# Router by column groups, state transposes in a gap, and two tiles' expert rows added by adding transfers: a change to a one-core hybrid decoder step

## The chip, the cores and the metric

One core of one Trainium2 chip runs the whole kernel. The metric is device time in microseconds of an execution; lower is better. The kernel before was timed in three runs, and one further execution was taken by the hardware profiler. Times of the trace are microseconds from the start of its span.

## What is computed

One layer over 512 prompt tokens and 32 sample tokens (8 sequences of 4), width 1024, all in float32. Cut to what the change touches:

```python
x = x + g1 * mix                          # mix: pooling and short convolution, then w_out
h2 = rmsnorm(x, norm2) * (1.0 + sc2) + sh2
logits = h2 @ w_router + b_router         # 32 experts
top_v, top_i = lax.top_k(logits, 4)
gates = softmax(top_v)
# every expert: down(((u + 1) * g * sigmoid(1.702 g))) + b_down on the rows that chose it
ffn = zeros.at[token].add(y_rows * gate)  # four rows a token
x = x + g2 * ffn
y = rmsnorm(x, final_norm)
```

Beside y it returns the last 15 rows of the pooling input and the last 2 rows of the convolution input, for the prompt and for the samples (the "states").

## The kernel before

The tokens are five tiles: four of 128 prompt tokens (t = 0 to 3) and one of 32 sample tokens (t = 4, `PT`). Each engine has its own program in a block of the dense part (to about 250 us) and in a block of the experts; they meet at semaphores, and within an engine the order is the written one. That order, not a planner, sets when things run.

**Dense part.** TensorE multiplies the output projection tile by tile (`mix(t)`, L1096, samples at L1092). VectorE gates and adds it into `x_sb` (L892, L893), ScalarE squares and takes the root, VectorE normalises into `h_row` (L741, L743), TensorE transposes that (`transposes`, L955) and ScalarE copies it out of PSUM as `h_t` (`turned`, L537). `router(t)` (L1108) multiplies `h_t` as the loaded operand, eight chunks of 128 by 128 tokens, with the 32 columns of `wr_sb`. A float32 product is two records in the trace. `best(t)` on VectorE (L866 to L874) adds the bias, takes the top 8, their indices, casts these to float (`top_f`, L870), and makes one-hot rows and a mask. The order on TensorE is h0, mix(2), h1, router(0), mix(3), h2, router(1), transposes of the prompt's last state columns into `acc_u` (L1139, L1141), mix(4), h3, router(2), router(3), the samples' rows, router(4), ranks (L1159 to L1163), transposes of the samples' state columns (L1168, L1170). `TP` names the uses of the PSUM buffer `tp` in order: TensorE counts `tp_full`, ScalarE `tp_free`. The normalised rows are stored to DRAM (`h2_dram`), tiles 0 to 2 by SP, tile 3 and the samples by ScalarE's queue.

**Experts.** An expert takes up to 96 rows of the normalised tokens (3 blocks `b` of 32), each row cut into 4 quarters that lie on the four groups of 32 partitions; TensorE works on four column groups at once. `row_ids(e)` (L2088) gives the indices of expert e's rows, VectorE's `ids(e)` (L1718 to L1723) turns them into addresses, and GpSimd gathers (L1549) one block at a time; VectorE transposes the rows (`turn_first` for expert 0 by block, L1735; `turn_rows`, L1742 and later). The first two experts get their indices in this way, the others from a table made of ranks and gates: pairs (L1892, L1905) on VectorE, `values_by_rank` (L2097) on TensorE, more of VectorE (to L1926), `values_by_slot` (L2105). TensorE's order at the start is row_ids(0), row_ids(1), g2 of the prompt (L2179), g2 of the samples (L2182), `keep_clock` (L2112, a product nobody reads), gate and up of expert 0 (L2124, L2146), values_by_slot, gate and up of expert 1. From there the loop is gate_up(i) (L2146, 192 records), down(i) (L2171, 192 records).

Weights go through 12 slots of 1 MB, in pairs of 2 MB from expert 1 on, on SP's queue (L1468), each load waiting for TensorE to have used the slots. Expert outputs, scaled by gate and g2, are scattered by GpSimd (L1562) as quarter rows into `expert_rows` in DRAM (`y_dram`), row 4 * token + k for the token's k-th choice. The outputs of the last two experts (`LATE`) stay in SBUF.

**End.** When all scatters but those of the last two experts have landed, SP loads the rows back (L1493, L1497): tiles 0 and 1 as `picked[0]`, `picked[1]` (2 MB each, a token's four rows side by side in one partition), tile 2, the samples and tile 3 with one row a partition into free weight slots. Tiles 0 and 1 are summed by VectorE (`add_pairs` L1788, `add_rows` L1793 and L1795), in its program around the last expert's `y_add` (L1772, L1776). TensorE takes the last two experts' rows to their tokens with a 0/1 matrix (`late_expert`, L2258, 48 records a tile) and, for tiles 2, 3 and the samples, adds the loaded rows by products with `sel_4`, which sums four neighbouring partitions (`other_experts`, L2269 to L2276). The tile order is `SEQUENCE = [0, 1, PT, 2, 3]`. VectorE adds each result to `x_sb` (`add_tile`, L1815; tile 3 by quarters, L1802), ScalarE squares (L1670), VectorE scales by `final_norm` (L1981, L1996), and the tiles are stored. `late_expert(3)` waits for the samples' root, since that sum and tile 3 share a PSUM bank.

Of the kernel before, what the change touches and what calls it, by code (L numbers as in the profile page):

```python
# [6 lines left out]
ALU = mybir.AluOpType  # L7
# [45 lines left out]
Q = 4  # L53
# [11 lines left out]
def hybrid_step(nc, x_prompt, x_sample, state_pool, state_conv, c_prompt, c_sample, norm1, norm2,  # L65
# [11 lines left out]
    with top:  # L77
# [127 lines left out]
        v_new = sb("v_new", [P, GR, DEC_B * CPAST])  # L205
        logit = sb("logit", [P, TT, E])
        top_i = sb("top_i", [P, TT, 8], U32)
        top_f = sb("top_f", [P, TT, TOPK])
# [27 lines left out]
        rank_ps = acc_y[:, 0, PT * E:(PT + TT) * E].rearrange("p (t e) -> p t e", e=E)  # L236
        ss_ps = acc_g[:, 1, 0:1]
# [17 lines left out]
        consts = sem("consts")  # L255
# [43 lines left out]
        TP += ["pm_s", "h0", "h1", "h2", "h3", "h4"]  # L299
# [85 lines left out]
        def _(sp):  # L385
# [23 lines left out]
            sp.wait_ge(so0_full, 1)  # L409
            sp.wait_ge(new_packed, 4)  # L410
# [6 lines left out]
        def _(pool):  # L417
# [9 lines left out]
            pool.memset(eps_c[:, :], EPS).then_inc(consts, 1)  # L427
            pool.memset(ss[:, :], 1.0).then_inc(consts, 1)
# [23 lines left out]
            for w in range(16):  # L452
                pool.memset(inv_n[:, w:w + 1], 1.0 / (w + 1)).then_inc(consts, 1)
            pool.memset(uext[:, :, 0:PAST], 0.0).then_inc(consts, 1)
            pool.memset(vext[:, :, 0:CPAST], 0.0).then_inc(consts, 1)
            pool.memset(top_v[:, :, :], 0.0).then_inc(consts, 1)
# [75 lines left out]
        def _(act):  # L532
# [28 lines left out]
            act.wait_ge(consts, 2)  # L561
# [95 lines left out]
            def states(i0, src):  # L657

                for i in (i0, i0 + 1):
# [8 lines left out]
                           vext_s[:, :, :, DEC_T:DEC_T + CPAST], ACT.Copy).then_inc(new_packed, 1)  # L668
            for t in range(PT):
# [8 lines left out]
                if t == 0:  # L678
# [11 lines left out]
            act.activation(rstd_q[:, :], ss_ps, ACT.Sqrt, bias=eps_c[:, 0:1], scale=1.0 / D).then_inc(sq_done, 1)  # L690
            store(PT - 1)
            empty(f"h{PT}", h_t[:, :, SEQ:NTOK].rearrange("p (q h) s -> p h q s", q=Q),
                  tp[:, 0, 0:QW].rearrange("p (h q s) -> p h q s", h=KT // Q, q=Q))
            act.wait_ge(h_ready, TT + PT + 1)
# [14 lines left out]
        def _(dve):  # L709
# [79 lines left out]
            dve.wait_ge(consts, CONSTS)  # L789
# [72 lines left out]
            def best(t):  # L862
# [57 lines left out]
        def _(pe):  # L920
# [179 lines left out]
            def router_part(t, lo_, hi_):  # L1100
                r = norm_rows(t)
                out_ = lg[t]
                if lo_ == 0:
                    pe.wait_ge(tp_free, TP[f"h{t}"] + 1)
                    if t >= 2:
                        pe.wait_ge(logits_in, t - 1)
                for k in range(lo_, hi_):
                    mm = pe.matmul(out_, h_t[:, k, t * P:t * P + r], wr_sb[:, k, :],  # L1108
                                   start=(k == 0), stop=(k == KT - 1))
                if hi_ == KT:  # L1110
                    mm.then_inc(lg_done, 1)

            def router(t):
                router_part(t, 0, KT)
# [15 lines left out]
            transposes("h1", 1, TT)  # L1130
            router(0)
            mix(3)
            transposes("h2", 2, TT)
            router(1)
            pe.wait_ge(pm_ready, 2 * GR)
            pe.wait_ge(conv_s_ready, GR)
            pe.wait_ge(x1_ready, PT)
            for g in range(GR):
                pe.transpose(acc_u[0:PAST, 0, g * P:(g + 1) * P], uext[:, g, SEQ:SEQ + PAST], ident[:, :])  # L1139
            for g in range(GR):  # L1140
                mm = pe.transpose(acc_u[0:CPAST, 1, g * P:(g + 1) * P], vext[:, g, SEQ:SEQ + CPAST], ident[:, :])  # L1141
            mm.then_inc(so0_full, 1)
            mix(4)
            transposes("h3", 3, TT)
            router_part(2, 0, KT // 2)
            pe.wait_ge(act_step, 2 * TT)
            pe.matmul(ss_ps, same_s[:, :], ss_q[:, 0:1], start=True, stop=True).then_inc(ss_summed, 1)
            router_part(2, KT // 2, KT)
            router(3)
            take("h4")  # L1150
# [4 lines left out]
            router(4)  # L1155
# [10 lines left out]
            pe.wait_ge(new_packed, 4)  # L1166
            for g in range(GR):
                pe.transpose(tp[0:NS, 0, g * P:(g + 1) * P], u_new[:, g, :], ident[:, :])  # L1168
            for g in range(GR):
                mm = pe.transpose(tp[0:DEC_B * CPAST, 1, g * P:(g + 1) * P], v_new[:, g, :], ident[:, :])  # L1170
            mm.then_inc(so_full, 1)
# [30 lines left out]
        with ExitStack() as experts:  # L1202
# [93 lines left out]
            quarter_done = sem("quarter_done")  # L1296
# [121 lines left out]
            picked_at = [picked[0], picked[1]] + [slots(n, 2).rearrange("p (k d) -> p k d", k=TOPK) for n in (0, 4, 6)]  # L1418
# [24 lines left out]
            def _(sp):  # L1443
# [37 lines left out]
                for t in (0, 1, 2, PT, 3):  # L1481
# [4 lines left out]
                    if t == 2:  # L1486
                        sp.wait_ge(mm_done, pos(E - 1, 2 * MCH - 1) + 1)
# [43 lines left out]
            def _(pool):  # L1531
# [7 lines left out]
                def gather_waits(e):  # L1539

                    pool.wait_ge(id_ready, e + 1)
                    if not (isinstance(e, int) and e == 0):
                        pool.wait_ge(ht_ready, e)
# [158 lines left out]
            def _(dve):  # L1702
# [94 lines left out]
                def add_tile(t):  # L1797
# [14 lines left out]
                    if t < AHEAD:  # L1812
                        dve.wait_ge(x_added, t + 1)
# [518 lines left out]
```

## Time and profile before

| | us |
|---|---|
| median of 3 runs | 1278.76 (1278.58 to 1279.07) |
| the profiled execution's own time | 1278.6 |
| its span in the trace | 1276.8 |
| TensorE busy | 1259.5 |
| VectorE busy | 522.0 |
| GpSimd busy | 250.0 |
| ScalarE busy | 92.8 |

In the rows, PE is TensorE's matmuls and PEld its loads of the stationary operand (the first shape in a row is that of the loaded operand), DVE is VectorE, ACT ScalarE, POOL GpSimd, SPq the DMA queue of SP. q1 is SP's hardware queue, q0 the one that GpSimd issues to. A row of the timeline merges instructions of one line that follow each other (x, a count); in square brackets stands the idle time of the engine before it and what ended it. Ends of matmuls are modelled, so starts are the surer numbers. The chain that ended last is followed back from the last instruction, each time to what released it.

### The profile page before, as it was taken

How to read it: one execution, taken by the hardware profiler on the slowest of the kernel's cores; microseconds unless marked ns; L12 is line 12 of the kernel's file. 1: busy time of each engine (PE TensorE's matmuls, PEld its weight loads, DVE VectorE, ACT ScalarE, POOL GpSimd, SP SyncE). 2: the span in 40 equal slices, each digit the busy share in tenths (PEclk: the TensorE clock that was granted, in tenths of full speed). 3: DMA queues.
4: the chain of work that ended last, by engine and by line, in shares of the span. 5: the costliest groups of instructions: out<-in, count | busy, mean ns of one | idle time of the engine just before them, and what ended most of it. 6: DMA issues, size and time to landing. Idle time of an engine off the chain costs nothing.

```text
span 1276.8 us, 32305 instructions
## 1 busy us (share of the span) xinstructions
PE 1259.5 (99%) x14181; PEld 587.5 (46%) x14181; DVE 522.0 (41%) x826; ACT 92.8 (7%) x184; POOL 250.0 (20%) x333
## 2 busy tenths in 40 slices
PE   8999999899999999999999999999999999999997
PEld 7777755533344334433443444444444444333445
DVE  2033323575333333333333344444444444444346
ACT  5110011200000000000000000000000000000002
POOL 4502300122222111111221111111111111112110
PEclk9999999799999999999999999999999999999999
DMA  9455968399999999999999999999999999999994
GB/s 349 138 210 214 354 247 335 101 392 426 423 428 428 426 427 426 425 428 425 428 424 424 428 424 419 426 426 427 423 417 429 424 424 429 422 425 427 426 423 176
DMA packets 62819, 487.60 MB, mean 382 GB/s; under 512 B 10563, under 2 KB 19635, under 8 KB 37441
## 3 DMA queue, kind: packets, MB, share of 16 engines
q1 hardware_dynamic: 47826, 455.79, 85.6%
q0 software_dynamic: 11632, 20.85, 4.6%
q10 hardware_dynamic: 3327, 10.47, 2.1%
q8 instruction: 25, 0.41, 0.1%
q14 instruction: 9, 0.07, 0.0%
HBM read 468.48 MB, written 25.88 MB: 387 GB/s over the span
## 4 chain that ended last, share of the span: by engine, by line
PE 94%; DVE 3%; DMA 1%; issue 1%; POOL 0%; ACT 0%; POOLq 0%; DVEq 0%; ACTq 0%
PE acc L2146 50%; PE acc L2171 24%; PE acc L1004 9%; PE acc L1096 4%; PE acc L934 2%; DMA rows<-h_rows,row_first 1%; PE acc L2258 1%; PE acc L978 1%; PE acc L955 1%; DVE picked L1788 0%; PE acc L1068 0%; PE acc L1092 0%; PE acc L1108 0%; POOL rows L1549 0%; PE acc L2273 0%
## 5 line engine op out<-in xcount | busy, mean ns | idle before, releaser
L2146 PE MATMUL acc<-raw,ht 128*32 128x512 f32 x2928 | 319.8, 592 | 0.0
L2146 PE MATMUL acc<-raw_b,ht 128*32 128x512 f32 x2928 | 319.8, 592 | 0.0
L1851 DVE TENSOR_TENSOR g_sb<-acc,bias_gu 128x768 f32<-128x768 f32 x32 | 30.7, 958 | 518.0 <-PE acc L2146 518.0
L1549 POOL DMA_INDIRECT rows<-h_rows,row_next x90 | 93.4, 1037 | 689.1 <-DVE row_next L1729 625.2
L2146 PEld LDWEIGHTS acc<-raw_b,ht 128*32 128x32 f32 x2928 | 95.0, 110 | 219.1 <-issue 219.1
L2146 PEld LDWEIGHTS acc<-raw,ht 128*32 128x32 f32 x2928 | 95.1, 110 | 205.7 <-issue 200.4
L2171 PE MATMUL acc<-raw_b,at 128*32 128x256 f32 x2976 | 166.3, 379 | 0.0
L2171 PE MATMUL acc<-raw,at 128*32 128x256 f32 x2976 | 166.3, 379 | 0.0
L2171 PEld LDWEIGHTS acc<-raw_b,at 128*32 128x32 f32 x2976 | 96.7, 110 | 77.1 <-issue 18.6
L2171 PEld LDWEIGHTS acc<-raw,at 128*32 128x32 f32 x2976 | 96.7, 110 | 63.9
L1004 PE MATMUL acc<-h_t,raw 128*128 128x256 f32 (+1 forms) x512 | 119.8, 395 | 0.4 <-DVE h_t L764 0.3
L1004 PEld LDWEIGHTS acc<-h_t,raw 128*128 128x128 f32 x512 | 96.6, 190 | 22.4 <-issue 2.6
L1562 POOL DMA_INDIRECT expert_rows<-y_sb,y_idx x90 | 91.6, 1018 | 75.1 <-DVE y_sb L1776 47.7
L1631 ACT ACTIVATE a_sb<-g_sb 128x768 f32<-128x768 f32 x32 | 27.1, 846 | 603.3 <-DVE g_sb L1853 603.3
L1751 DVE STREAM_TRANSPOSE at<-a_sb 128x768 f32<-128x768 f32 x31 | 49.7, 1603 | 27.6 <-PE acc L2171 27.6
L1742 DVE STREAM_TRANSPOSE ht<-rows 128x768 f32<-128x768 f32 x30 | 48.0, 1601 | 0.8 <-DMA rows<-h_rows,row_next 0.8
L1762 DVE TENSOR_SCALAR weight<-g_q,table 128x256 f32<-128x256 f32 x96 | 33.8, 408 | 4.9 <-issue 4.9
L1624 ACT ACTIVATE y_idx<-table,q_col 128x3 uint32 (+1 forms) x30 | 9.0, 298 | 318.5 <-DVE y_sb L1772 318.5
L1776 DVE TENSOR_TENSOR y_sb<-y_sb,weight 128x768 f32<-128x768 f32 x31 | 29.7, 959 | 3.5
L1863 DVE SCALAR_TENSOR_TENSOR a_sb<-u_sb,g_sb 128x768 f32<-128x768 f32 x32 | 30.7, 959 | 1.1
L1859 DVE TENSOR_TENSOR g_sb<-g_sb,a_sb 128x768 f32<-128x768 f32 x32 | 30.5, 952 | 0.0
L1854 DVE TENSOR_TENSOR u_sb<-acc,bias_gu 128x768 f32<-128x768 f32 x32 | 30.4, 951 | 0.0
(296 smaller groups left out, 694.4 us busy)
## 6 DMA issues: line engine op xcount, KB each, us to landing
raw<-in_w_down SPq DMA_DIRECT2D x33, 2048.0 KB, 16.9
raw<-in_w_gate SPq DMA_DIRECT2D x31, 2048.0 KB, 11.7
raw<-in_w_up SPq DMA_DIRECT2D x31, 2048.0 KB, 16.1
raw_b<-in_w_gate SPq DMA_DIRECT2D x31, 2048.0 KB, 11.2
raw_b<-in_w_up SPq DMA_DIRECT2D x31, 2048.0 KB
raw_b<-in_w_down SPq DMA_DIRECT2D x31, 2048.0 KB, 16.5
raw<-in_w_ada SPq DMA_DIRECT2D x24, 1024.0 KB, 10.5
expert_rows<-zeros ACTq DMA_DIRECT2D x1, 8704.0 KB, 29.0
```

What stands on the lines that cost most here:

```text
L1004: mm = pe.matmul(z_half(f, b), w[:, j, (f % 2) * P:(f % 2 + 1) * P], h_t[:, j, lo_:hi_], start=(j == 0), stop=(j == KT - 1))
L1096: mm = pe.matmul(out_[0:r, h, :], mix_t[j][:, t * P:t * P + r], w[:, j % KC, h * HALF:(h + 1) * HALF], start=(j == GR), stop=(j == GR - 1))
L1549: pool.indirect_dma_start(rows[:, b, :], None, h2_quarter, bass.IndirectOffsetOnAxis(ap=idx[:, b:b + 1], axis=0), bounds_check=Q * NTOK - ...
L1562: pool.indirect_dma_start(y_quarter, bass.IndirectOffsetOnAxis(ap=y_idx[:, b:b + 1], axis=0), y_sb[:, b, :], None, bounds_check=Q * ROWS - ...
L1742: dve.transpose(ht_of(e)[:, :, :, :], turned(rows)).then_inc(ht_ready, 1)
L1751: dve.transpose(at_[:, :, :, :], turned(a_sb)).then_inc(at_ready, 1)
L1762: dve.tensor_scalar(weight[:, b, :], g2_q[:, :], in_prompt, in_sample, ALU.mult, ALU.add)\
L1851: dve.tensor_tensor(g_sb[:, :, :], gate_of(i, 0), plus(0), ALU.add).then_inc(g_read, 1)
L1859: dve.tensor_tensor(g_sb[:, :, :], g_sb[:, :, :], s_sb[:, :, :], ALU.mult).then_inc(glu_done, 1)
L1863: dve.scalar_tensor_tensor(out=a_sb[:, :, :], in0=u_sb[:, :, :], scalar=1.0, in1=g_sb[:, :, :], op0=ALU.add, op1=ALU.mult).then_inc(act_re ...
L2146: mm = pe.matmul(gu_of(i)[b][q * TB:(q + 1) * TB, :].rearrange("p (m n) -> p m n", m=2), ht_of(i)[:, b, k, :], w[:, kk, :, q * CW:(q + 1) ...
L2171: mm = pe.matmul(out_[q * TB:(q + 1) * TB, b, :], x[:, b, k, :], w[:, kk, q * CW:(q + 1) * CW], start=(k == 0), stop=(k == KT - 1))
```

## The change

- Router: `router_parts(t)` loads `wr_sb` chunks (32 columns) as the stationary operand into column group k mod 4 and moves `h_t` (128 tokens) past it, giving four partial sums of 32 logits in the four partition groups. ScalarE copies them (`partial_sums`), and `router_fold(t)` sums the four groups with one product with `same_s`. `TP` gets the names r0 to r4. The fold stands behind the next tile's transposes.
- `best(t)` compares with the integer indices and has no cast.
- The prompt's last state columns are copied by ScalarE into `end_cols`; their transposes and those of the samples' states move from the dense part to behind row_ids(0), ahead of row_ids(1). `keep_clock` moves ahead of both g2 products, and g2 of the samples goes between blocks 0 and 1 of expert 0's first products.
- On VectorE the gates subtraction moves behind the members of expert 1, and ids(1) ahead of turn_first. GpSimd's gathers for expert 1 wait for each block of expert 0 to be turned, no longer for all of them.
- Tiles 2 and 3: GpSimd adds the four rows a token straight to `x_sb` with `dma_start(..., accum_op=add)`, eight transfers of 512 KB, each waiting for the one before of its tile; the first two are issued with SP's first loads of the rows, the others behind the last expert's gate and up. SP's loads of these tiles and TensorE's `other_experts` for them go; tile 3 is added whole and no longer by quarters.
- The semaphore `consts` is merged into `rows_cleared`; SP waits for six packings before its third load of experts.

```diff
@@ ScalarE, dense part
+            def partial_sums(t):
+                empty(f"r{t}", part_sb[t], part_ps[t])
...
+            act.activation(end_cols[:, :, 0:PAST], uext[:, :, SEQ:SEQ + PAST], ACT.Copy).then_inc(new_packed, 1)
+            act.activation(end_cols[:, :, PAST:PAST + CPAST], vext[:, :, SEQ:SEQ + CPAST], ACT.Copy)\
+                .then_inc(new_packed, 1)
...
+                if t:
+                    partial_sums(t - 1)
                 if t < PT - 1:
                     turned(f"h{t}", t)
@@ TensorE, dense part
+            def router_parts(t):
+                r = norm_rows(t)
+                pe.wait_ge(tp_free, TP[f"h{t}"] + 1)
+                if t >= 2:
+                    pe.wait_ge(logits_in, t - 1)
+                for k in range(KT):
+                    g = k % Q
+                    mm = pe.matmul(part_ps[t][g * E:(g + 1) * E, :], wr_sb[:, k, :], h_t[:, k, t * P:t * P + r],
+                                   start=(k < Q), stop=(k >= KT - Q))
+                mm.then_inc(tp_full, 1)
+            def router_fold(t):
+                pe.wait_ge(tp_free, TP[f"r{t}"] + 1)
+                pe.matmul(lg[t], part_sb[t], same_s[:, 0:E], start=True, stop=True).then_inc(lg_done, 1)
...
             mix(2)
-            transposes("h1", 1, TT)
-            router(0)
+            router_parts(0)
+            row_transposes(1)
+            router_fold(0)
             mix(3)
...
@@ VectorE, best(t)
-                step(dve.tensor_copy(top_f[0:r, t, :], top_i[0:r, t, 0:TOPK]))
                 step(dve.tensor_tensor(onehot[0:r, t, :, :], iota_e[0:r, :].unsqueeze(1).to_broadcast([r, TOPK, E]),
-                                       top_f[0:r, t, :].unsqueeze(2).to_broadcast([r, TOPK, E]), ALU.is_equal))
+                                       top_i[0:r, t, 0:TOPK].unsqueeze(2).to_broadcast([r, TOPK, E]), ALU.is_equal))
@@ SP, end
-                for t in (0, 1, 2, PT, 3):
+                for t in (0, 1, PT):
...
-                    if t == 2:
-                        sp.wait_ge(mm_done, pos(E - 1, 2 * MCH - 1) + 1)
@@ GpSimd, experts
+                    if isinstance(e, int) and e == 1:
+                        pool.wait_ge(first_turned, b + 1)
...
+                def add_rows(t, k):
+                    rows_ = y_dram[TOPK * P * t:TOPK * P * (t + 1), :].rearrange("(p k) d -> k p d", k=TOPK)
+                    if k:
+                        pool.wait_ge(rows_added[t - AHEAD], 16 * k)
+                    pool.dma_start(x_sb[:, t, :], rows_[k], accum_op=ALU.add).then_inc(rows_added[t - AHEAD], 16)
+
+                pool.wait_ge(y_stored, 16 * SB * (E - LATE))
+                for t in range(AHEAD, PT):
+                    add_rows(t, 0)
                 pool.wait_ge(mm_done, pos(E - 1, 2 * MCH - 1) + 1)
                 pool.iota(tokno, pattern=[[Q, NTOK]], base=0, channel_multiplier=0,
                           allow_small_or_imprecise_dtypes=True).then_inc(numbered, 1)
+                for k in range(1, TOPK):
+                    for t in range(AHEAD, PT):
+                        add_rows(t, k)
@@ VectorE, add_tile(t)
-                    if t == LAST:
-                        for q in range(Q):
-                            dve.wait_ge(quarter_done, q + 1)
...
+                    else:
+                        dve.wait_ge(rows_added[t - AHEAD], 16 * TOPK)
@@ TensorE, start of the experts
                 row_ids(0)
+                end_states()
+                sample_states()
                 row_ids(1)
+                keep_clock()
                 pe.wait_ge(so_ready, 4)
...
-                keep_clock()
                 gate_up_first()
```

## Rows read from the trace of the kernel before

**Rows 1.** The page, part 1: busy time, share of the span, instructions, per engine.

```profile
PE 1259.5 (99%) x14181; PEld 587.5 (46%) x14181; DVE 522.0 (41%) x826; ACT 92.8 (7%) x184; POOL 250.0 (20%) x333
```

**Rows 2.** Waits of SP's queue, 290 to 1240 us: us in total, times, longest.

```profile
SPq L1468 <- PE acc L2146: 570.9, 61, 12.0
```

**Rows 3.** Chain, 200 to 340 us: start, us, engine and line, instructions.

```profile
214.16 1.71 PE acc L1108 x16
...
233.38 3.64 PE acc L1092 x64
...
246.29 0.85 PE acc L1168 x4
...
248.00 0.62 PE acc L2088 x44
...
279.81 20.74 PE acc L2146 x192
```

**Rows 4.** Timeline, 237 to 248 us: start, us, instruction, [idle before, releaser].

```profile
237.04 0.42 DVE L905 TENSOR_TENSOR h_q<-acc,g_q 128x256 f32<-128x256 f32 x1 [0.30 <-PE acc L1092]
...
240.98 0.17 DVE L870 CAST top_f<-top_i 128x4 f32<-128x4 uint32 x1
...
242.20 0.19 DVE L866 TENSOR_TENSOR logit<-acc,br_bc 128x32 f32<-128x32 f32 x1 [0.31 <-DVE mask_bf L874]
...
246.78 0.66 DVE L1712 TENSOR_TENSOR member<-iota_m,rank_m 128x480 bf16<-128x480 f32 x1
```

**Rows 5.** Windows: start:end, length, TensorE busy us, clock share, DMA share, GB/s.

```profile
252.00:256.00 4.00, 4.00 (x18) 0.53 0.37 105
```

**Rows 6.** Timeline, 254 to 279 us.

```profile
254.22 11.23 PE L2124 MATMUL acc<-raw_b,ht 128*32 128x512 f32 x96
...
262.48 4.16 DVE L1905 TENSOR_TENSOR picked<-onehot,pair_v 128x3840 bf16<-128x3840 f32 x1
...
263.09 4.43 POOL L1549 DMA_INDIRECT rows<-h_rows,row_first  x1 [0.30 <-issue]
...
273.51 1.61 DVE L1742 STREAM_TRANSPOSE y_sb<-rows 128x768 f32<-128x768 f32 x1 [6.87 <-DMA rows<-h_rows,row_first]
...
278.90 0.91 PE L2105 MATMUL acc<-picked,sel_r 96*128 96x96 f32 x6 [1.23 <-DVE picked L1926]
```

**Rows 7.** Timeline, 1248 to 1270 us.

```profile
1248.00 2.29 DVE L1788 TENSOR_TENSOR picked<-picked 128x2048 f32<-128x2048 f32 x1
...
1250.20 0.95 DVE L1772 TENSOR_TENSOR u_sb<-acc,bias_d 128x768 f32<-128x768 f32 x1
...
1262.70 1.93 PE L2273 MATMUL acc<-raw_b,sel 128*32 128x256 f32 x32
...
1263.30 0.49 DVE L1996 SCALAR_TENSOR_TENSOR raw<-x_sb,fin_rstd,fn_q 128x256 f32<-128x256 f32 x1
...
1267.37 1.93 PE L2273 MATMUL acc<-raw_b,sel 128*32 128x256 f32 x32
...
1268.15 1.65 DVE L1802 TENSOR_TENSOR x_sb<-x_sb,acc 128x256 f32<-128x256 f32 x4 [0.51 <-PE acc L2273]
```

**Rows 8.** DMA, 1229 to 1234 us; then the queues (packets, MB) 1218.0 to 1219.3.

```profile
DMA packets 147, 2.15 MB, mean 429 GB/s; under 512 B 16, under 2 KB 16, under 8 KB 16
...
q1 hardware_dynamic: 34, 0.51, 91.5%
q0 software_dynamic: 33, 0.08, 15.9%
```

**Rows 9.** Tile `picked`, 1200 to 1277 us: issues, and issue to landing.

```profile
L1493 SPq DMA_DIRECT2D picked<-expert_rows x2: 326/350/373, 1223.0 to 1223.4; - x2
...
DMA to landing us min/median/max: 16.5/18.7/20.9
```

**Rows 10.** Tile `raw`, 1215 to 1225 us: issues, and issue to landing.

```profile
L1468 SPq DMA_DIRECT2D raw<-in_w_down x2: 342/380/418, 1219.1 to 1219.5; - x2
...
DMA to landing us min/median/max: 10.6/12.8/15.1
```

More of the change, by code:

```diff
@@ L236, in hybrid_step @@
         rank_ps = acc_y[:, 0, PT * E:(PT + TT) * E].rearrange("p (t e) -> p t e", e=E)
+        part_ps = [acc_y[:, t % 2, 3 * P:3 * P + (NS if t == PT else P)] for t in range(TT)]
+        part_sb = [gate_c[:, 2 + t % 2, 0:NS if t == PT else P] for t in range(TT)]
         ss_ps = acc_g[:, 1, 0:1]
@@ L1098, in mix, with row_transposes @@
                 mm.then_inc(mix_done, 1)
-            def router_part(t, lo_, hi_):
+            def router_parts(t):
                 r = norm_rows(t)
[L1102 to L1114, printed above, removed]
+                pe.wait_ge(tp_free, TP[f"h{t}"] + 1)
[9 more added lines that the diff above has]
+                pe.matmul(lg[t], part_sb[t], same_s[:, 0:E], start=True, stop=True).then_inc(lg_done, 1)
+            def row_transposes(t):
+                transposes(f"h{t}", t, TT, tp, TP[f"h{t - 1}"] + 1)
             pe.wait_ge(conv_ready, GR - 1)
@@ L1129, in _ @@
             mix(2)
-            transposes("h1", 1, TT)
-            router(0)
+            router_parts(0)
+            row_transposes(1)
+            router_fold(0)
             mix(3)
-            transposes("h2", 2, TT)
-            router(1)
+            router_parts(1)
+            row_transposes(2)
+            router_fold(1)
             pe.wait_ge(pm_ready, 2 * GR)
             pe.wait_ge(conv_s_ready, GR)
[L1137 to L1142, printed above, removed]
             mix(4)
-            transposes("h3", 3, TT)
-            router_part(2, 0, KT // 2)
+            router_parts(2)
+            row_transposes(3)
+            router_fold(2)
             pe.wait_ge(act_step, 2 * TT)
             pe.matmul(ss_ps, same_s[:, :], ss_q[:, 0:1], start=True, stop=True).then_inc(ss_summed, 1)
-            router_part(2, KT // 2, KT)
-            router(3)
-            take("h4")
+            router_parts(3)
+            router_fold(3)
+            pe.wait_ge(tp_free, TP["h3"] + 1)
             pe.wait_ge(h_ready, TT + PT + 1)
@@ L1154, in _ @@
             mm.then_inc(tp_full, 1)
-            router(4)
+            router_parts(4)
+            router_fold(4)
             pe.wait_ge(mask_ready, 1)
@@ L1164, in _ @@
             mm.then_inc(rank_done, 1)
[L1166 to L1171, printed above, removed]
         part.close()
@@ L1295, in hybrid_step @@
             tile_done = sem("tile_done")
-            quarter_done = sem("quarter_done")
+            rows_added = [sem(f"rows_added{t}") for t in range(2)]
             fin_cross = sem("fin_cross")
@@ L1414, in blocks @@
                     again()
-            picked_at = [picked[0], picked[1]] + [slots(n, 2).rearrange("p (k d) -> p k d", k=TOPK) for n in (0, 4, 6)]
+            picked_at = {0: picked[0], 1: picked[1], PT: slots(6, 2).rearrange("p (k d) -> p k d", k=TOPK)}
             beside = slots(2, 2)
@@ L1541, in gather_waits @@
                     pool.wait_ge(id_ready, e + 1)
-                    if not (isinstance(e, int) and e == 0):
+                    if not isinstance(e, int) or e > 1:
                         pool.wait_ge(ht_ready, e)
@@ L1873, in _ @@
                 dve.wait_ge(rows_zeroed, 16)
-                dve.tensor_tensor(gates[:, :, :], top_v[:, :, 0:TOPK], top_v[:, :, 0:1].to_broadcast([P, TT, TOPK]),
-                                  ALU.subtract).then_inc(shifted, 1)
                 chain(dve.scalar_tensor_tensor(out=rank_m[:, :, :], in0=rank_ps, scalar=1.0, in1=mask_bf[:, :, :],
@@ L1882, in _ @@
                 members(1)
+                dve.tensor_tensor(gates[:, :, :], top_v[:, :, 0:TOPK], top_v[:, :, 0:1].to_broadcast([P, TT, TOPK]),
+                                  ALU.subtract).then_inc(shifted, 1)
                 chain(dve.tensor_tensor(pick[:, :, :, :], onehot[:, :, :, :],
@@ L2180, in _ @@
                 mm.then_inc(g2_spread, 1)
-                for q in range(Q):
-                    mm = pe.matmul(g2_s_ps[q * NS:(q + 1) * NS, :], sel_s[:, q, :], mod_g2[:, :], start=True, stop=True)
-                mm.then_inc(g2_spread, 1)
-                keep_clock()
                 gate_up_first()
```

82 lines of the change are left out of this document (45 added, 37 removed).

## The prediction

> **What bounds the kernel now.** The page first: TensorE has work in 99% of the span and VectorE in 41% [rows 1]. Weights stream all the while too, so the wait table of SP's own queue has to say who paces whom: through the experts the weight loads wait for TensorE's matmuls to free a slot [rows 2], and in the table of the engines TensorE waits for no load. An expert's gate and up are 20.74 us of products back to back [rows 3]; the change touches neither these nor the down products. It can act only where the chain leaves them: between the output projection and expert 1's first product (214 to 280 us), and behind the last down product (1250 us on). I read the chain of waits there, then the timeline for what stands beside it.
>
> **Front, step by step.**
>
> 1. Router. A tile's 8 products take 1.71 us on the chain, 16 records that each load 128 columns [rows 3]. `router_parts` loads 32 columns, four groups at once, with 128 moving columns. Nearest is mix(4): 64 such records with 256 moving columns in 3.64 us, 0.057 each. 16 of them give 0.91, half of that if the moving columns set it; I take 0.6. The fold adds two records at the old price (0.11 each): 0.2. So a tile saves 0.9 (0.6 to 1.05). The ACT copy between is hidden by the next row transposes and an idle ACT; without that cover it would cost its own 0.3.
> 2. Only router(0) stands ahead of mix(3), so tile 3's sum starts 0.9 earlier; `best(1)` on VectorE's way loses its cast (0.17 and 0.03 of issue), 1.1. Before, VectorE waited 0.30 at L905 for mix(4) [rows 4]; mix(4) moves up by two router tiles, 1.8, and by the state transposes, so the wait goes and VectorE leads. h_q: 1.4 earlier.
> 3. `best(2)` to `best(4)` follow back to back: three casts, 0.6, and the 0.3 of idle at 242.20 [rows 4]. The masks are ready 2.3 earlier.
> 4. Expert 0's members are made at 247.44 [rows 4], but their ids start at 248.00, behind two groups of transposes of 0.85 each [rows 3], which now stand behind them: 0.5. The gates subtraction leaves this path too, which I count as nothing. The first gather goes out 2.8 earlier; its rows are turned at about 251.1.
> 5. What is late next is TensorE: 0.62 of ids, then 16 transposes (twice the two groups, 3.4), ids(1) 0.6 to 0.8, `keep_clock` and g2 of the prompt (1.7 and 0.85 at the slow clock, half at the full one). From 245.2 that ends between 251.2 and 252.6. First product at 251.9 against 254.22: 2.3 gained, bounds 1.6 and 3.1. SP's loads of slots 4 and 5 start behind the first gathers and move up with them; 10 us of products cover them.
> 6. Clock. Between 252 and 256 the grant was 0.53 of full, that is mostly 1.2 GHz [rows 5], after the router steps in which VectorE leads and TensorE waits. The first 96 records took 11.23 us [rows 6] where 96 of the same shape take 10.37 (half of 20.74): 0.9 lost. With TensorE busy from 245 on I expect it back (bounds 0 and 0.9). Against it g2 of the samples enters the products: 0.43.
> 7. Expert 1's gathers were asked for at 258.5; the third one's issue alone took 4.43 us beside a 4.16 us product of pairs on VectorE, its rows came at 273.5, and TensorE stood 1.23 us before L2105 [rows 6]. With ids(1) ahead of `turn_first` the indices are there at about 250.4 (when row_ids(1) leaves TensorE), and the gathers follow block by block; with the same landing of some 10 us they are there by 268. VectorE then reaches the slot values near 270, TensorE needs them at 275. The 1.23 goes.
>
> Front: 2.3 + 0.9 - 0.4 + 1.2 = 4.0 us; with the bounds of steps 1, 5 and 6, 2.4 to 4.8. The copies into `end_cols`, the merged semaphore and SP's wait for six packings hang on engines long idle there: nothing.
>
> **Tail, the gain.** other_experts(2) and the quarters of tile 3 leave TensorE (1.9 each). Tile 3's late products ran from 1264.6 to 1267.4, VectorE's last quarter ended at 1269.80 [rows 7]. Now they wait for the samples' root (1263.1) and end at 1265.9, and VectorE is what is late: samples finished at 1263.8 [rows 7], add of tile 2 1.22, weighting 1.23, root and reciprocal to 1266.8, add of tile 3 1.22: 1268.0. Gain 1.8; what follows is unchanged.
>
> **Tail, the price.** GpSimd issues eight adding transfers of 512 KB, two at once with SP's loads of `picked` (1223.0), the others from 1230, each behind its tile's last. SP's two 2 MB loads for tiles 2 and 3 go, but they were queued behind both picks and delayed nothing; the adds are on a queue of their own. Where both queues had work, 34 packets went on one and 33 on the other: turn by turn [rows 8]. A 16 KB packet of the stream costs an engine 0.61 us (131 in 5 us on 16 engines: 147 less the 16 small ones) [rows 8], one of 4 KB a quarter of that, 0.15. From the first add to the second pick's landing, 1244.2 [rows 9], the stream sends some 30 packets an engine, and a 4 KB row of the adds goes behind each. Who waits: add_pairs(1) on VectorE starts at 1248.00, 3.8 us behind that landing, and right behind it is the last expert's y_add, which today starts the moment the last down product is out (1250.20) [rows 7]. Every microsecond beyond 3.8 delays the end.
>
> No row shows an adding packet. Lower bound: a plain one, 0.15, 4.5 in all, 0.7 beyond the slack (none at all is a rival below). Upper bound: x is read as well, so two reads of 4 KB, 0.30: 9.0, 5.2 beyond. A plain packet is the nearest row, the second read is the nearest mechanism; I take the middle, 0.22: 6.6, 2.8 beyond. By then four adds are done; the rest run alone at some 5 us a pair and end near 1260, ahead of 1263.8. The weights of the last down products landed by 1234.6 [rows 10]; these products end at 1250.2 and take half of an expert's gate and up, so they need them from 1239.8 on: covered, 3 us later too.
>
> **Sum.** -4.0 - 1.8 + 2.8 = -3.0 on the profiled execution's 1278.6 (span 1276.8); the median of the runs is 0.16 above it, 1278.76: 1275.7.
>
> **A rule against the change.** GpSimd's issue was held for 4.43 us beside VectorE's tensor_tensor [rows 6], so an add's issue beside add_pairs (2.3) may be held as long. While the queue is full that is hidden; it counts for the third rival. The Trainium skill (SBUF — State Buffer, "Who interferes with whom") infers that tensor_tensor leaves descriptor writing alone and that copies and tensor_scalar lock it out. By its inference that issue would not have been held; the row decides.
>
> **Rivals.**
> - *The picks are not late* (0.18). If the adds get less than every second turn, the slack covers them: -4.0 - 1.8, 1272.9. For: adds of one tile are chained, so their queue may run dry. Against: two tiles interleave, and the other queue's packets did get every turn.
> - *Adds too dear, slower* (0.25). Place: add_pairs(1) waiting for `picked[1]`. From 0.32 us an adding packet the whole gain is gone; at 0.45 (row read, x read, x written one after another) the delay is 13.5, 9.7 beyond the slack: 1278.8 - 5.8 + 9.7 = 1282.7.
> - *The adds themselves late* (0.12). If a 4 KB row goes as several packets, each waits its own 0.61 us: at two, 10 to 12 us a transfer, two are done by 1247, six remain in three rounds of 5 to 6 us, 1263 to 1266. With picks little delayed that is 1 to 3 us late: 1274 to 1276. The Trainium skill (DMA: Bandwidth & Descriptors, "Anatomy of one DMA") fits 2.0 us plus bytes at 436 GB/s; an estimate by it is 3.2 us per add, the last one near 1243, and nobody would wait for it.
> - *The front gives less* (0.10). ids(1) now holds `turn_first` on VectorE until TensorE is through 3.4 us of transposes; if these run late and the clock stays low, the front gives 2: 1277.7.
>
> The forecast has 0.35. 0.2% is 2.6 us, about what a measurement of this kernel can tell from no change. Faster: two thirds of the forecast (0.23; its own range is 1273.5 to 1278.5, the bounds of the packet and some of the front's), the first rival, most of the third: 0.51. Slower: nearly all of the second: 0.24. Between: 0.25. The range takes 1272.9 from the first rival and 1282.7 from the second.
>
> **What would show it.** L905 at 235.6; the first L2124 record between 251 and 253 and a full grant before 256; no idle before the slot values; expert 1's first L2146 near 275.8. In the tail, `picked` landing in 21 and 27 us instead of 16.5 and 20.9; VectorE idle before add_pairs(1), y_add 2.8 later against the last down product; no wait for `rows_added`. The prediction is wrong if VectorE waits at `rows_added`, if the picks land in time, or if TensorE waits for a load of the last expert.

## The result, and the profile after

The changed kernel takes **1281.82 us** (median of 11 runs, 1280.19 to 1282.33) beside 1278.77 us for the kernel before (1277.97 to 1279.45) on the same chip: ratio 1.0021, 95% interval 1.0013 to 1.0029. Forecast were 1275.7 us, and faster. The profiled execution has a span of 1279.6 us, against 1276.8 before: +2.8.

**The front did what was forecast, less 0.6 us.** The chain of waits of the changed kernel, 200 to 340 us (start, duration, engine and line, instructions), answers to [rows 3] and, at `h_q`, to the first row of [rows 4]:

```profile
235.58 0.43 DVE h_q L915
...
239.47 0.64 PE acc L1126 x2
...
245.57 0.62 PE acc L2127 x46
...
250.26 1.76 PE acc L2151 x2
...
252.59 3.43 PE acc L2165 x32
...
276.38 20.74 PE acc L2187 x192
```

Expert 1's first product starts at 276.38 where it started at 279.81: 3.43 gained, 4.0 forecast. Through the 30 experts that follow the gain neither grows nor shrinks, since nothing in them was changed. Three rows from the timeline of the same kernel (start, duration, instruction, idle time before it and its releaser) answer to [rows 4] and [rows 6]; the fourth is from the table of windows (length, busy of PE, PEld, DVE, ACT, POOL, then granted clock, DMA share, GB/s) and answers to [rows 5]:

```profile
242.24 0.18 DVE L877 TENSOR_TENSOR logit<-acc,br_bc 32x32 f32<-32x32 f32 x1 [0.52 <-PE acc L1126]
...
256.03 2.46 POOL L1557 DMA_INDIRECT rows<-h_rows,row_first  x1 [0.31 <-issue]
...
264.51 1.61 DVE L1764 STREAM_TRANSPOSE y_sb<-rows 128x768 f32<-128x768 f32 x1 [0.90 <-DMA rows<-h_rows,row_first]
...
252.00:256.00 4.00, 4.00 (x45) 1.41 (x48) 2.87 (x5) 1.50 (x2) 3.12 (x4) 1.00 0.46 114
```

The reader is to see three things: the grant is full from 252 on where it was 0.53 up to 256; the third gather of expert 1 takes 2.46 us to issue and not 4.43; and its rows are turned at 264.5 and not 273.5, so TensorE no longer stops ahead of the slot values.

**The tail gave back twice the gain.** First the timeline of the changed kernel from 1236 us on, which answers to [rows 7]:

```profile
1236.36 0.97 DVE L1794 TENSOR_TENSOR y_sb<-acc,bias_d 128x768 f32<-128x768 f32 x1
...
1242.99 2.29 DVE L1810 TENSOR_TENSOR picked<-picked 128x2048 f32<-128x2048 f32 x1 [3.04 <-DMA picked<-expert_rows]
...
1251.46 2.29 DVE L1810 TENSOR_TENSOR picked<-picked 128x2048 f32<-128x2048 f32 x1 [3.66 <-DMA picked<-expert_rows]
...
1253.67 0.95 DVE L1794 TENSOR_TENSOR u_sb<-acc,bias_d 128x768 f32<-128x768 f32 x1
...
1255.67 2.95 PE L2298 MATMUL acc<-u_sb,raw_b 32*128 32x256 f32 x24 [7.53 <-DVE u_sb L1798]
...
1271.54 1.22 DVE L1832 TENSOR_TENSOR x_sb<-x_sb,acc 128x1024 f32<-128x1024 f32 x1
```

Both `add_pairs` on VectorE wait for their pick, 3.04 and 3.66 us, and the last expert's y_add stands behind the second. Measured from the start of the slot values, y_add comes 1253.67 - 275.47 = 978.2 us later; before it is 1250.20 - 278.90 = 971.3. That is 6.9 us lost, and no other stretch loses as much. Then the landing of `picked` and all packets and the queues from 1225 to 1230 us (packets, MB, share of 16 engines), which answer to [rows 9] and [rows 8]:

```profile
DMA to landing us min/median/max: 23.3/27.3/31.3
...
DMA packets 176, 1.69 MB, mean 338 GB/s; under 512 B 7, under 2 KB 7, under 8 KB 95
...
q1 hardware_dynamic: 88, 1.33, 64.2%
q0 software_dynamic: 88, 0.36, 36.9%
```

88 packets of each queue: turn by turn, as forecast. The 7 packets under 512 B carry almost no bytes; 95 less 7 leaves 88 of 4 KB, which is the whole adding queue. But 36.9% of 16 engines over 5 us is 29.5 us for 88 adding packets, **0.34 us each**, above even my upper bound of 0.30. The count was right. From the first adding packet (1224.1) to the last 16 KB packet of the picks (1249.15) the adding queue moved 1.98 MB, that is 484 packets of 4 KB or 30 an engine, as forecast.

The sum in the trace: first product -3.4, y_add behind it +6.9, and from y_add to the end 25.9 us where it was 26.6, -0.7: +2.8, the difference of the spans.

### The profile page after: what moved, and what is told of

Same layout as the page of the kernel before. It is cut to its first block, busy times and chain, and to the rows that moved or that the text cites. A ratio compares the mean times of both kernels' runs of the same rounds, so it can differ in the third digit from the quotient of the medians.

```text
span 1279.6 us, 32201 instructions
## 1 busy us (share of the span) xinstructions
PE 1252.9 (98%) x14127; PEld 583.9 (46%) x14127; DVE 520.1 (41%) x818; ACT 94.3 (7%) x191; POOL 255.3 (20%) x341
## 4 chain that ended last, share of the span: by engine, by line
PE 93%; DMA 4%; DVE 1%; ACT 1%; issue 1%; SPq 0%; POOL 0%; DVEq 0%; POOLq 0%; ACTq 0%
PE acc L2187 49%; PE acc L2212 24%; PE acc L1014 9%; PE acc L1106 4%; DMA picked<-expert_rows 2%; PE acc L944 2%; PE acc L2298 1%; PE acc L2165 1%; DMA x_sb<-in_x_prompt 1%; DMA expert_rows<-y_sb,y_idx 1%; PE acc L965 0%; PE acc L1078 0%; ACT junk L558 0%; DVE x_sb L1832 0%; ACT raw L1692 0%
## 5 line engine op out<-in xcount | busy, mean ns | idle before, releaser
L1798 DVE TENSOR_TENSOR y_sb<-y_sb,weight 128x768 f32<-128x768 f32 x31 | 29.7, 958 | 3.5
## 6 DMA issues: line engine op xcount, KB each, us to landing
raw_b<-in_w_down SPq DMA_DIRECT2D x31, 2048.0 KB, 17.7
```

## Experiments

Each ratio is against the kernel before on the same chip. "y_add" is the last expert's y_add counted from the start of the slot values, as above; 971.3 is on time.

**1 and 2. The change cut in two.** `front_only` has the hunks of routing and gap and keeps the tail of the kernel before, with tiles 2 and 3 loaded by SP and added by TensorE; `tail_only` has only the new tail, shown here in part, and the merged semaphore:

```
-                for t in (0, 1, 2, PT, 3):
+                for t in (0, 1, PT):
...
+                pool.wait_ge(y_stored, 16 * SB * (E - LATE))
+                for t in range(AHEAD, PT):
+                    add_rows(t, 0)
...
+                for k in range(1, TOPK):
+                    for t in range(AHEAD, PT):
+                        add_rows(t, k)
```

> The changed kernel with the end of the kernel before: tiles 2 and 3 loaded by SP and added by TensorE, no adding transfers. My theory: the front of the change is worth what its trace shows, 3.4 us (expert 1's first product at 276.4 in place of 279.8), and the loss is all in the tail: 1275.3 us against 1278.8. Rival (the shifted front makes the tail late, for instance because weights of the last experts come closer to their use): 1278 or more.

> The kernel before with the new end alone (adding transfers, whole tile 3), and the merged semaphore. My theory: the adds hold back the loads of picked by 7 and 10 us of which 3.8 are covered, so y_add of the last expert comes 6.9 us late; of the 1.8 us that the end gains, 1.3 go to a halved clock of the first late products: +6.4, 1285.2 us. Rival (front and tail hurt one another): about 1280, with the rest of the loss seen only in the two together.

Measured: front alone 1274.50 us, ratio 0.9970 (0.9958 to 0.9981); tail alone 1283.59, ratio 1.0038 (1.0025 to 1.0050). So -4.1 and +5.0; together +0.9, where the whole change measures +3.0. Of the 2.1 between them the traces show 1.0: the front gains 4.1 in `front_only` and 3.4 in the whole change, and y_add is 6.6 late in `tail_only` and 6.9 there; the rest is within the intervals. For the tail alone I had expected 6.4; its trace shows 6.0 (span 1282.8), in an execution 1.0 above the median of its runs. With the front alone the first product starts at 275.69, y_add is on time, and the picks land after 17.2, 19.4 and 21.7 us. The tail alone shows the whole loss by itself:

```profile
DMA to landing us min/median/max: 22.4/26.6/30.8
...
1254.41 2.29 DVE L1799 TENSOR_TENSOR picked<-picked 128x2048 f32<-128x2048 f32 x1 [4.02 <-DMA picked<-expert_rows]
...
1258.62 2.94 PE L2264 MATMUL acc<-u_sb,raw_b 32*128 32x256 f32 x24 [7.20 <-DVE u_sb L1787]
```

**3. Is it the adding, or only the extra transfers?** In `adds_plain` the same eight transfers go at the same places but copy (the addition itself is left out):

```
-                    pool.dma_start(x_sb[:, t, :], rows_[k], accum_op=ALU.add).then_inc(rows_added[t - AHEAD], 16)
+                    pool.dma_start(x_sb[:, t, :], rows_[k]).then_inc(rows_added[t - AHEAD], 16)
```

> The changed kernel with the eight transfers of GpSimd as plain copies into the same tiles of x_sb, same bytes, same places, same waits (tiles 2 and 3 then hold an expert's row instead of x plus four rows). Theory A, the price is the addition: a 4 KB packet costs an engine 0.15 us instead of 0.35, picked lands 3 and 5 us later than before instead of 7 and 10, y_add about 1 us late, the clock stays: 1274.5 to 1275.5 us. Theory B, the price is the turn that any second queue takes from the stream: as the changed kernel, 1281.8 us.

Measured: 1275.69 us, ratio 0.9976 (0.9966 to 0.9985). Landing of `picked`, and all packets and the queues from 1225 to 1230 us:

```profile
DMA to landing us min/median/max: 20.6/23.5/26.3
...
DMA packets 232, 2.06 MB, mean 411 GB/s; under 512 B 30, under 2 KB 30, under 8 KB 132
...
q1 hardware_dynamic: 115, 1.64, 79.5%
q0 software_dynamic: 117, 0.42, 21.1%
```

Here 30 packets are under 512 B, 15 of them in q0, so the copies are 132 less 30, 102 packets of 4 KB. 21.1% of 80 us over 102 is 0.165 us, a little above the lower bound of 0.15. Both queues still take turns, and a turn of the second one costs half of what it does with adds: **an adding packet takes as long as two plain ones of its size**. 1281.82 - 1275.69 = 6.1 us of the kernel's time are due to the adding alone; for the extra transfers as such VectorE still waits 0.43 and 1.30 us for the picks, and y_add is 1.9 late where I had expected about 1.

**4. No adds at all.** `no_adds` is the changed kernel without the eight transfers and VectorE's wait for them (the other experts' rows of tiles 2 and 3 are left out).

> The changed kernel with the eight adding transfers left out (tiles 2 and 3 then lack the rows of the experts but the last two). This has the gain of the tail without its price. My theory: picked lands as before, y_add starts with the last product, late products keep the clock, the end gains the 1.8 us of the prediction: front 3.5 to 4.1 and tail 1.8 below the kernel before, 1272.8 to 1273.4 us. Rival (the new end gains nothing by itself, VectorE's whole adds eat it): as the front alone, 1274.5.

Measured: 1273.31 us, ratio 0.9954 (0.9937 to 0.9970), as expected. The queue from 1225 to 1230 us, the landing, and the last add:

```profile
q1 hardware_dynamic: 150, 2.18, 102.3%
...
DMA to landing us min/median/max: 17.1/19.3/21.5
...
1263.71 1.22 DVE L1824 TENSOR_TENSOR x_sb<-x_sb,acc 128x1024 f32<-128x1024 f32 x1
```

This is the size of the prize: y_add on time, and VectorE's last add ends 1264.93 - 1247.25 = 17.7 us after it, where it was 19.6 before [rows 7]. The tail gain was forecast at 1.8 and is 1.9. The adds cost 1281.82 - 1273.31 = 8.5 us.

**5. Fewer adds, and half adds.** `two_adds` keeps only each tile's first add and leaves out the other six; `adds_half` keeps all eight but moves 512 of the 1024 columns and leaves out the rest:

```
-                    pool.dma_start(x_sb[:, t, :], rows_[k], accum_op=ALU.add).then_inc(rows_added[t - AHEAD], 16)
+                    pool.dma_start(x_sb[:, t, 0:D // 2], rows_[k][:, 0:D // 2],
+                                   accum_op=ALU.add).then_inc(rows_added[t - AHEAD], 16)
```

> Only the first add of each tile is left (two of eight; the other three rows a token of tiles 2 and 3 are left out): 16 adding packets an engine instead of some 27 to 30 ahead of the second pick. Theory A (each adding packet ahead of the picks delays them by its 0.36 us, VectorE has 3 us of slack): second pick lands 27 us after its issue (21.5 + 5.8), y_add 2.5 to 3 us late: 1275.5 to 1277. Theory B (the delay comes from the chained adds that come later, or from something they do to the queue beside their packets): the picks land at 22 us and the time is that without adds, 1273.3.

> Every add moves only the first 512 of the 1024 columns: 2 KB packets instead of 4 KB, as many of them, turn by turn with the stream as before (the second half of the columns of tiles 2 and 3 lacks the rows of the experts). It tells whether the adding packet is paid by its bytes or by its count. Without adds the second pick landed 21.5 us after its issue and the kernel took 1273.3; with the full adds 31.3 us and 1281.8. Theory A, price by bytes (0.36 us at 4 KB, so 0.18 at 2 KB): half the delay, second pick at 26 to 27 us, y_add 2 us late instead of 7: 1275 to 1276.5. Theory B, a fixed price for each packet (0.36 whatever its size): 31 us and 1281 to 1282. Between the two, a fixed part and a part by bytes: the landing tells the split.

Measured, on a chip where the kernel before takes 1280.71 us: 1278.10, ratio 0.9983 (0.9974 to 0.9993), and 1278.18, ratio 0.9983 (0.9973 to 0.9992). The times are above what I expected, for a reason at the front (experiment 9). The part that was to be tested stands in the landings. Of `adds_half`, the landing and the queues from 1236 to 1241 us:

```profile
DMA to landing us min/median/max: 18.5/21.4/24.3
...
q1 hardware_dynamic: 108, 1.61, 76.8%
q0 software_dynamic: 108, 0.22, 23.6%
```

23.6% of 80 us over 108 packets is 0.17 to 0.18 us at 2 KB (one of the 108 is a small one), half of the 0.34 at 4 KB: **an adding packet is paid by its bytes**. The delay fell more than by half (2.8 us and not 4.9). Ordered by it:

| | price of a packet on q0, us | second pick lands after, us | y_add, us |
|---|---|---|---|
| no_adds | none | 21.5 | 971.3 |
| adds_half | 0.18 | 24.3 | 972.0 |
| two_adds | 0.33, half as many | 24.7 | 971.9 |
| adds_plain | 0.165 | 26.3 | 973.2 |
| changed kernel | 0.34 | 31.3 | 978.2 |

The changed kernel run a second time (experiment 9) has its second pick at 32.4 and y_add at 979.4, so a difference of a few tenths between two rows says nothing. Up to a landing of about 24 us less than 1 us is lost; of the 7.0 us by which the second pick comes later in the changed kernel than in `adds_half`, y_add takes over 6.2. `two_adds` fell short of its expected 27 us: 16 packets an engine at 0.33 are 5.3 us, and the pick came 3.2 later. Both the price and the count (256 packets) are in the trace; where the other 2 us went no run shows. In the changed kernel the sum comes out: 30 packets at 0.335 are 10.0 us, and the pick came 9.8 later than without adds.

**6. Could the adds wait until the picks are in?** `adds_last` issues all eight behind both picks' landing; `tile3_adds` is `front_only` with tile 3 alone served by four adds there, tile 2 by TensorE as before. The lines of `adds_last`:

```
+                pool.wait_ge(tile_in[0], 32)
+                pool.wait_ge(tile_in[1], 32)
+                for k in range(TOPK):
```

> The changed kernel with all eight adds issued only when both picked tiles have landed. My theory: picked lands in 16.5 and 20.9 us as before and y_add starts with the last product; the adds then run from about 1241 on without the stream at 0.35 us a packet, four pairs of 6 us, so the last of tile 2 lands near 1263 and of tile 3 near 1266, 2 to 3 us after they are needed: 1276 to 1277 us. Rival (an adding transfer is slow by itself, whatever stands beside it, with 10 us each): 1290 or more.

> The front of the change with adding transfers for tile 3 alone, four of them, issued when both picked tiles have landed; tile 2 is loaded by SP and added by TensorE as before. By the runs so far a chained pair of adds takes 7.4 us without the stream, so one alone some 5: four end near 1262 to 1264, with the load of tile 2's rows beside them; tile 3's late products end near 1263.3. My theory: 0 to 1.1 us under the front alone, 1273.4 to 1274.5 us. Rival (tile 2's rows are held back by the adds as picked was, TensorE waits for them): 1276 or more.

Both expectations missed: 1285.74 us, ratio 1.0054 (1.0037 to 1.0071), and 1282.69, ratio 1.0026 (1.0016 to 1.0036). The second pick landed after 21.5 and 21.8 us and y_add was on time in both. But the chain of adds was last. The timeline of `adds_last`:

```profile
1242.67 1.96 POOL L1617 DMA_DIRECT2D x_sb<-expert_rows  x2 [15.69 <-DMA picked<-expert_rows]
...
1268.54 0.87 POOL L1617 DMA_DIRECT2D x_sb<-expert_rows  x1 [3.18 <-DMA x_sb<-expert_rows]
...
1272.12 1.22 DVE L1831 TENSOR_TENSOR x_sb<-x_sb,acc 128x1024 f32<-128x1024 f32 x1 [11.40 <-DMA x_sb<-expert_rows]
```

Then `tile3_adds`, with the issue to landing of its four adds:

```profile
1266.61 0.87 POOL L1622 DMA_DIRECT2D x_sb<-expert_rows  x1 [6.50 <-DMA x_sb<-expert_rows]
...
1274.02 1.22 DVE L1827 TENSOR_TENSOR x_sb<-x_sb,acc 128x1024 f32<-128x1024 f32 x1 [8.93 <-DMA x_sb<-expert_rows]
...
DMA to landing us min/median/max: 6.6/7.2/8.8
```

I had counted 5 to 6 us for a pair. One add alone takes 7.2 us from issue to landing, a pair 7.4: two in flight cost hardly more than one, so more than half of it is not the packets (8 an engine at the 0.39 that they take alone are 3.1 us) but some 4 us, by subtraction, that every link of the chain pays anew. With four links a tile, that is 30 us. Nobody can wait for that behind the picks. The Trainium skill (DMA: Bandwidth & Descriptors, "Anatomy of one DMA") gives 2.0 us plus bytes at 436 GB/s, 3.2 us for such a transfer by my estimate; the measured 7.2 decides, and the page's fit does not hold for the adding transfers here.

**7. The clock behind the wait.** TensorE stands 7.5 us for y_add, then the 24 records of its first late products take 2.95 us where they took 1.58. `kept_warm` is the changed kernel with 30 products into an unused bank that fill this wait (of their 60 records the trace has 45):

```
+                for _ in range(30):
+                    pe.matmul(psum[:, 3, CW:CW + P], ident[:, :], ident[:, :], start=True, stop=True)
```

> The changed kernel with 30 products of ident on ident, read by nobody, ahead of TensorE's wait for the last y_add, where it now idles 7.5 us. My theory: the grant stays full, the first late products of the last expert take 1.5 us again in place of 2.95, and 1.2 us of the loss come back: 1280.5 us. Rival (the late products were not on the path, VectorE was): 1281.8, no change.

Measured: 1279.42 us, ratio 1.0003 (0.9994 to 1.0013). First the window and the late product of the changed kernel, then, in a second fence, of `kept_warm`:

```profile
1255.00:1257.00 2.00, 1.33 (x12) 1.19 (x16) 1.97 (x3) 0.00 (x0) 0.55 (x1) 0.50 0.84 127
```

```profile
1255.00:1257.00 2.00, 1.30 (x24) 1.25 (x28) 1.97 (x3) 0.00 (x0) 0.53 (x1) 1.00 0.82 129
...
1249.78 5.19 PE L2321 MATMUL acc<-ident 128*128 128x128 f32 x45
...
1255.70 1.58 PE L2298 MATMUL acc<-u_sb,raw_b 32*128 32x256 f32 x24 [0.73 <-DVE u_sb L1798]
```

At a grant of 0.50 (1.2 GHz) 12 records fit where 24 do at 1.00 (2.4 GHz). With the clock kept, VectorE's last add ends 1271.38 - 1253.70 = 17.7 us behind y_add, the same as without adds; in the changed kernel it is 19.1. So the late picks cost 1.4 us a second time, through the clock. The medians differ by more, 2.4 us, but the intervals of the two ratios leave room for 1.4.

**8. Which part of the front carries it?** `ids_back` is `front_only` with `ids(1)` and its gathers where they were, behind `turn_first`:

```
-                ids(1)
                 turn_first()
                 gate_up_bias(0)
+                ids(1)
```

> The front of the change alone, but ids(1) again behind turn_first and the bias, and the gathers of expert 1 behind all blocks. Step 7 of the prediction gave this 1.2 us. My theory: expert 1's rows land some 7 us later than in the front alone, VectorE is late with the slot values and TensorE idles there again, 1.2 us or a little more since TensorE comes 3 us earlier: 1275.7 to 1277 us. Rival (the 1.23 us of idle hung on something else, such as the pairs on VectorE): 1274.5.

Measured: 1277.03 us, ratio 0.9982 (0.9972 to 0.9992), 2.5 above the front alone. The timeline:

```profile
260.21 4.16 DVE L1911 TENSOR_TENSOR picked<-onehot,pair_v 128x3840 bf16<-128x3840 f32 x1
...
260.89 4.35 POOL L1557 DMA_INDIRECT rows<-h_rows,row_first  x1 [0.30 <-issue]
...
271.44 1.61 DVE L1750 STREAM_TRANSPOSE y_sb<-rows 128x768 f32<-128x768 f32 x1 [7.08 <-DMA rows<-h_rows,row_first]
```

The third gather is again issued beside the 4.16 us product of pairs and again takes over 4 us, and TensorE waits 1.96 us ahead of the slot values. The order of `ids(1)`, with the gathers that follow it, is thus worth 2.5 of the front's 4.1 us. I had given it 1.2 in step 7. The wait is longer here, and it costs clock as well: from 276 to 280 us the grant is 0.61, where it is 1.00 with the front alone, and the slot values take 1.57 instead of 0.91 us.

**9. Does the front's gain hold?** In the traces of `two_adds` and `adds_half` the slot values started 4.6 and 4.9 us later than in the changed kernel, whose front they share. Of `two_adds`, TensorE's timeline and one window:

```profile
249.95 0.50 PE L2124 MATMUL acc<-tok_bf,member 128*32 128x2 bf16 x45
250.93 0.23 PE L2124 MATMUL acc<-tok_bf,member 128*32 128x2 bf16 x5 [0.48 <-issue]
251.67 0.22 PE L2124 MATMUL acc<-tok_bf,member 128*32 128x2 bf16 x5 [0.51 <-issue]
...
252.00:256.00 4.00, 3.60 (x19) 1.25 (x23) 2.98 (x8) 1.50 (x2) 2.31 (x5) 0.50 0.40 91
```

`row_ids(1)` runs in pieces with stretches of half a microsecond for which nothing in the trace stands, and the grant stays at 0.50 to 256 and beyond. So both kernels were run again unedited.

> The changed kernel again, nothing edited, beside the next one. In the two runs with half adds and with two adds, TensorE's row_ids(1) ran in pieces with three idle stretches of 0.5 us that nothing in the trace releases, the grant stayed at 0.50 until about 257 us and expert 1's first product stood at 281 us in place of 276; on that chip before itself took 1280.7. Theory A: those pauses come and go between chips and executions. Then this run shows either first product near 276.4 and ratio 1.002, or near 281 and ratio 1.004 to 1.006. Theory B: they belong to those two programs (where their instructions lie): first product near 276.4 and a ratio of 1.002 here on any chip.

> The front half alone again, nothing edited, to learn whether its gain holds on other chips. Theory A (pauses come and go): ratio 0.997 where row_ids(1) runs in one piece, 1.000 to 1.001 where it runs in pieces and the grant comes back late. Theory B (they belong to the other two programs): ratio 0.997 again, expert 1's first product at 275.7.

Measured: 1281.73 us, ratio 1.0017 (1.0008 to 1.0027), and 1274.48, ratio 0.9965 (0.9953 to 0.9978). No pauses; the first product starts at 276.7 and 275.6. Both results hold, though the second trace of the changed kernel is 2.5 us longer than the first (span 1282.1), in an execution 2.2 above the median of its runs. The pauses stand in these two traces alone, and both are of one chip, where the kernel before was 1.6 to 2.1 us slower too; whether they belong to that chip or to the two programs stays open, since no other kernel with this front ran on it.

## Why the prediction was wrong

The forecast had both halves and the place of the loss right, one price wrong and one cost missing: the result lies at +3.0 where the forecast said -3.0.

- **Router, casts, ids (steps 1 to 4).** `h_q` forecast at 235.6, measured 235.58. The masks 0.4 later than forecast (243.64 for 243.2): for tile 4 fold, ScalarE's copy and partial sums became a chain of their own, and `best(4)` waits 0.52 us for it. I had called the copy hidden; ahead of the last tile its cover is gone.
- **First products (step 5).** 252.6 for 251.9, the upper of the bounds: those 0.4, and 0.3 for TensorE's work up to there at the lower clock. The clock itself (step 6) came back as forecast. With the slot values free of their wait (step 7), 276.4 for 275.8. Front: -3.4 for -4.0.
- **Tail gain.** 1.8 forecast, 1.9 in the kernel without adds.
- **Tail price: the step that failed.** "I take the middle, 0.22: 6.6, 2.8 beyond" the slack. The turns (every second one) and the count (30 an engine) were right. The price was not: 0.335 us, just beyond the upper bound of 0.30, which I had built as two plain reads. Two plain packets of `adds_plain` are 0.33. The mechanism behind that bound, x being read as well, gives the measured price whole, though no run shows that a second read is what takes the time; the middle between it and the lower bound had no mechanism at all. 30 at 0.335 are 10.0 us where I had 6.6. The second pick came 9.8 us later than without adds, and y_add 6.9. By the forecast's own threshold, 0.32 us, the gain was gone; I gave that rival 0.25 and it was the case. Only its size was off: it had 9.7 at 0.45 us.
- **What I had not priced at all.** The clock of the first late products behind a long wait, 1.4 of the 1.9 of the tail gain.
- **The miss, added up in the trace.** 5.8 us: 0.6 at the front, 4.1 at y_add and 1.1 behind it. Of the 4.1, 3.4 are the price; the rest goes with the second pick, which even without adds lands 21.5 us after its issue and not 20.9. The 1.1 is the clock, less the 0.1 that the tail gained beyond its forecast, within 0.2.
- **The adds' own pace.** I wrote 5 us for a pair running alone. A pair takes 7.4. In the changed kernel that did not show, since VectorE never waits at `rows_added`; it sank both repairs.
- **The issue beside `add_pairs`.** I had feared that VectorE's tensor_tensor holds the issue of an add for as long as a gather's. It does not: the add issued at 1253.35, 0.40 us ahead of the end of the second `add_pairs`, took 0.88 us and did not wait for that end; the one at 1260.26, with VectorE idle, took 0.87. Of the other rivals the first and the third did not come: the picks were late, the adding packets stayed at 4 KB, and VectorE never waited at `rows_added`; the front gave 3.4 and not the 2 of the fourth.

What would have gone otherwise: at 0.22 us a packet the sum would be -3.4 + 2.8 - 1.9 = -2.5, near the forecast. This is reckoned from the measured front, the forecast's own delay and the tail gain without adds; no run has that price.

The version that beats both kernels is the front half alone: 1274.5 us, twice.

## What to carry over

A transfer that adds is not a copy: where it shares the 16 DMA engines with a stream that others wait for, count its packets by the stream's turns and price each at two plain packets of its size, and where it is chained count its latency, not its bytes. When a price lies between two mechanisms, take one of them and give the other its chance; their middle is the price of neither. An operation that no row shows is best measured first. And when a wait ahead of TensorE grows to several microseconds, add what the first products cost at half the clock.

## What the runs showed of the hardware

- An adding packet from DRAM into SBUF takes 0.335 us of a DMA engine at 4 KB and 0.18 at 2 KB, a plain one of 4 KB 0.165. Alone on the queues, at 1256 to 1260 us of the changed kernel, it is no cheaper: of 175 packets 16 are under 512 B, and 97.4% of 64 us over the other 159 is 0.39.

```profile
DMA packets 175, 0.65 MB, mean 163 GB/s; under 512 B 16, under 2 KB 16, under 8 KB 175
...
q0 software_dynamic: 175, 0.65, 97.4%
```

- One adding transfer of 512 KB takes 7.2 us from issue to landing (median of four), one of a pair 7.4 (median of eight); the fastest plain one of that size in `adds_plain` took 4.2. Of what the rest beyond the packets consists no run shows.
- Two queues share an engine by packets, not by bytes: 88 to 88 with 16 KB on one (but for 7 small ones) and 4 KB on the other. So each foreign packet costs the stream the time that it takes itself.
- GpSimd's issue of an indirect gather takes 4.43 and 4.35 us when it falls beside VectorE's 4.16 us tensor_tensor, and 2.46 beside one of 2.12 us, where it takes 1.0 to 1.2 otherwise. Each time it ends 0.87 or 0.88 us after the tensor_tensor. These three have bf16 output, but that is not the reason: among the experts of the changed kernel the gather issued at 620.01 beside an f32 one (`y_sb`, L1798, until 620.80) takes 1.70 and ends 0.90 after it. All four read both inputs from SBUF. The direct adding transfers are not held, as said above. The Trainium skill (SBUF — State Buffer, "Who interferes with whom") infers that tensor_tensor leaves descriptor writing alone, and the 0.88 us of a direct issue agree; it also says that a VectorE instruction with two inputs in SBUF contends with a GpSimd instruction that reads SBUF. A gather takes its row numbers from SBUF (`row_first`, `row_next`), so the held issues agree with that; that this read is what waits is argued, not shown.
